# Depthwise-convolution blocks of a Mamba layer: 256-channel halves over four k-tiles, the high and low token parts side by side in one matmul, and the first tap on GpSimd

## The reference

```python
def causal_depthwise_conv(x, w, bias):
    y = lax.conv_general_dilated(x, w[:, None, :], window_strides=(1,),
        padding=[(SSM_CONV - 1, 0)], dimension_numbers=('NWC', 'WIO', 'NWC'),
        feature_group_count=x.shape[-1])
    return y + bias

def mamba2_mixer(proj, conv_w, conv_b, dt_bias, a_log, d_skip, gate_norm):
    z, xbc, dt = jnp.split(proj, [SSM_D_INNER, SSM_D_INNER + SSM_CONV_DIM], axis=-1)
    xbc = jax.nn.silu(causal_depthwise_conv(xbc, conv_w, conv_b))   # 4096 channels, 4 taps
    xs, bm, cm = jnp.split(xbc, [SSM_D_INNER, SSM_D_INNER + SSM_BC], axis=-1)
    dt = jax.nn.softplus(dt + dt_bias)
    ...
```

## Time and profile before

| | |
|---|---|
| median of 3 runs | 1771.86 us (1771.59 to 1771.89) |
| the profiled execution | 1771.1 us, its span 1769.3 us |
| granted TensorE clock | 1.00 over the whole span |
| PE busy | 1763.4 us of the span |
| DVE, ACT, POOL busy | 1162.1, 1004.8, 220.8 us |
| the two convolution stages | 57.8 to 212.4 us (layer 0), 1291.5 to 1446.2 us (layer 3) |

### The profile page before, as it was taken

One profiled execution on the slowest core, in us unless ns is written; L12 is line 12 of the kernel. 1 busy time (PEld: TensorE's weight loads), 2 busy tenths in 40 slices (PEclk: granted clock), 3 DMA queues, 4 the chain that ended last, 5 costly groups with the idle time before them and its releaser, 6 DMA issues.

```text
span 1769.3 us, 25818 instructions
## 1 busy us (share of the span) xinstructions
PE 1763.4 (100%) x9492; PEld 1519.9 (86%) x9492; DVE 1162.1 (66%) x1596; ACT 1004.8 (57%) x1598; POOL 220.8 (12%) x548
## 2 busy tenths in 40 slices
PE   9999999999999999999999999999999999999999
PEld 8998988888888888888888888888899998888887
DVE  5788875655665665666666546666678887556665
ACT  6667775544455675544465545444566777545443
POOL 3412231000012230000012300000131223100000
PEclk9999999999999999999999999999999999999999
DMA  8565543566555443565655445666556554356663
GB/s 285 165 209 183 179 144 124 176 199 191 191 175 176 161 143 119 181 200 190 189 192 196 161 131 174 199 190 193 182 169 205 184 165 156 129 190 191 190 191 131
DMA packets 90041, 314.03 MB, mean 177 GB/s; under 512 B 10176, under 2 KB 11584, under 8 KB 89920
## 3 DMA queue, kind: packets, MB, share of 16 engines
q1 hardware_dynamic: 89328, 311.27, 54.4%
q10 hardware_dynamic: 592, 1.12, 0.2%
HBM read 311.23 MB, written 1.11 MB: 177 GB/s over the span
## 4 chain that ended last, share of the span: by engine, by line
PE 96%; DVE 2%; ACT 1%; issue 0%; DMA 0%; SPq 0%; DVEq 0%; ACTq 0%
PE ps L1229 19%; PE ps L1231 19%; PE ps L1230 19%; PE ps L1251 13%; PE ps L1258 7%; PE ps L1240 3%; PE ps L1241 3%; PE ps L1242 3%; PE ps L1396 2%; PE ps L1376 2%; PE ps L1327 1%; PE ps L1276 1%; PE ps L1286 1%; DVE w_lo_t L1669 1%; DVE xsT L1752 1%; DVE bcT L1752 1%
## 5 line engine op out<-in xcount | busy, mean ns | idle before, releaser
L1669 DVE TENSOR_TENSOR w_lo_t<-raw,w_hi_t 128x1024 fp32r<-128x1024 f32 x569 | 691.9, 1226 | 387.9 <-ACT w_hi_t L1425 387.4
L1425 ACT ACTIVATE w_hi_t<-raw 128x1024 fp32r<-128x1024 f32 x569 | 597.0, 1060 | 394.6 <-PE ps L1231 146.9
L1229 PE MATMUL ps<-w_hi_t,act_hi 128*128 128x512 f32 x832 | 329.2, 396 | 0.0
L1230 PE MATMUL ps<-w_lo_t,act_hi 128*128 128x512 f32 x832 | 324.2, 390 | 0.0
L1231 PE MATMUL ps<-w_hi_t,act_lo 128*128 128x512 f32 x832 | 324.1, 389 | 0.0
L1251 PE MATMUL ps<-hT,w_hi_t 128*128 128x512 f32 x1024 | 256.0, 392 | 0.0
L1251 PEld LDWEIGHTS ps<-hT,w_hi_t 128*128 128x128 f32 x1024 | 185.9, 189 | 34.4
L1231 PEld LDWEIGHTS ps<-w_hi_t,act_lo 128*128 128x128 f32 x832 | 156.2, 188 | 33.1
L1229 PEld LDWEIGHTS ps<-w_hi_t,act_hi 128*128 128x128 f32 x832 | 156.4, 188 | 31.2 <-issue 0.4
L1230 PEld LDWEIGHTS ps<-w_lo_t,act_hi 128*128 128x128 f32 x832 | 156.4, 188 | 30.6
L1229 PE MATMUL ps<-w_hi_t,hT 128*128 128x512 f32 x416 | 165.7, 398 | 0.0
(11 more groups left out here) (219 smaller groups left out, 2220.7 us busy)
## 6 DMA issues: line engine op xcount, KB each, us to landing
raw<-in_wstream SPq DMA_DIRECT2D x569, 512.0 KB, 3.8
gap<-cs_rows SPq DMA_DIRECT2D x32, 256.0 KB, 4.7
mix<-in_mem SPq DMA_DIRECT2D x4, 256.0 KB, 4.9
x<-in_x SPq DMA_DIRECT2D x1, 1024.0 KB, 9.3
raw<-in_wstream SPq DMA_DIRECT2D x2, 256.0 KB, 3.7
wsT<-in_sgu_wT ACTq DMA_DIRECT2D x1, 512.0 KB, 5.4
sgain<-in_sgu_gain ACTq DMA_DIRECT2D x1, 512.0 KB, 6.4
out<-x SPq DMA_DIRECT2D x1, 512.0 KB, 2.8
```

Source lines behind the costliest of these rows:

```text
L1229: pe.matmul(o, ah, wh[:, n], start=first and c == 0, stop=False)
L1230: pe.matmul(o, ah, wl[:, n], start=False, stop=False)
L1425: act.activation(w_hi_t[:, u % RING, :], raw[:, u % RING, :], ACT.Copy).then_inc(w_hi, 1)
L1669: dve.tensor_tensor(w_lo_t[:, u % RING, :], raw[:, u % RING, :], w_hi_t[:, u % RING, :].bitcast(F32), ALU.subtract)\
```

## The change

A block of 512 channels becomes two halves of 256 channels. Each half has two units of four k-tiles (`plan.halves`), form `half`, and takes one of the two pairs of banks; a bank holds one 128-channel tile, high tokens' product in the first 256 columns and low tokens' in the second. A new step `conv_sum` follows each half at once: ACT copies the second halves of the two banks into the new tile `cv`, DVE adds the first halves into `cv` (this frees the banks), and GpSimd multiplies `cv` by the last tap and adds the bias. The step `conv` on DVE then adds the other three taps from `cv` instead of from PSUM, when GpSimd's tap is there. A half unit's weights are loaded by two DMAs of 256 KB with runs of 1 KB instead of one DMA of 512 KB with runs of 4 KB. ACT's two first taps of 256 columns go.

```diff
-            self.block("feat", "hT", w, DIN + ft * P, job, taps)
+            u0 = len(self.units)
+            for half in range(2):
+                job = self.stream_job(True, True)
+                for n in range(2):
+                    u = len(self.units)
+                    self.halves[u] = (u0 + 2 * n, half)
+                    self.unit("half", "hT", (w, 2 * UK * half + UK * n, DIN + ft * P), job, n == 0, n == 1, self.parts["hT"][2 * n + 1], 4 * n,
+                              then=(lambda: half_summed(ft, half, job)) if n else None)
...
+        def half_summed(ft, half, job):
+            if 0 < ft < 16 and half == 0:
+                self.until(lambda: ft // 4 - 1 in xs_act)
+            n = self.count("conv")
+            self.until(lambda: n < 3 or self.n.get("taps", 0) >= n - 2)
+            job.read_act(self)
+            job.read_dve(self)
+            self.step("conv_sum", l=l, ft=ft, half=half, job=job, n=n, xs_free=xs_act[ft // 4 - 1] if 0 < ft < 16 else 0)
+            self.spawn(taps(ft, half, n))
...
+                    for k in range(2):
+                        at = slice(k * UK * 2 * P, (k + 1) * UK * 2 * P)
+                        sp.dma_start(raw[:, u % RING, at].rearrange("p (c f) -> p c f", c=UK),
+                                     A["wstream"][first + k].rearrange("p (c f) -> p c f", c=UK)[:, :, c]).then_inc(raw_in[u % RING], 16)
...
+                elif k == "conv_sum":
+                    h = s["half"]
+                    dst = xsT if s["ft"] < 16 else bcT[:, s["ft"] - 16:s["ft"] - 12, :]
+                    pool.wait_ge(pc_in, 32)
+                    pool.wait_ge(dve_free, s["job"].dve)
+                    if s["xs_free"]:
+                        pool.wait_ge(act_free, s["xs_free"])
+                    for f in range(2):
+                        c = s["l"] * TAPS * 32 + 3 * 32 + s["ft"] + 2 * h + f
+                        ins = pool.tensor_scalar(dst[:, 2 * h + f, :], cv[:, h, f, :], col("conv_w", c), col("conv_b", s["l"] * 32 + s["ft"] + 2 * h + f),
+                                                 ALU.mult, ALU.add)
+                    ins.then_inc(conv_tap, 1)
...
+                    elif s["form"] == "half":
+                        for q in range(4):
+                            for f in range(2):
+                                o, n = ps[:, job.banks[f], :], slice(q * 2 * P + f * P, q * 2 * P + (f + 1) * P)
+                                pe.matmul(o.rearrange("p (a b) -> p a b", a=2), wh[:, n], hT2[:, :, s["at"] + q, :], start=first and q == 0, stop=False,
+                                          skip_group_check=True)
+                        for q in range(4):
+                            for f in range(2):
+                                o, n = ps[:, job.banks[f], :], slice(q * 2 * P + f * P, q * 2 * P + (f + 1) * P)
+                                mm = pe.matmul(o[:, 0:SEQ], wl[:, n], hT2[:, 0, s["at"] + q, :], start=False, stop=last and q == 3,
+                                               skip_group_check=True)
...
-                elif k == "conv":
-                    job, h = s["job"], s["half"]
-                    dst = xsT if s["ft"] < 16 else bcT[:, s["ft"] - 16:s["ft"] - 12, :]
+                elif k == "conv_sum":
+                    job, b = s["job"], s["job"].banks[0]
                     act.wait_ge(job_done, job.done)
...
+                    if s["n"] > 2:
+                        act.wait_ge(conv_done, s["n"] - 2)
+                    act.activation(cv[:, s["half"], :, :], ps[:, b:b + 2, SEQ:2 * SEQ], ACT.Copy).then_inc(act_free, 1)
...
+                elif k == "conv_sum":
+                    job, b, c = s["job"], s["job"].banks[0], cv[:, s["half"], :, :]
+                    dve.wait_ge(act_free, job.act)
+                    dve.tensor_tensor(c, ps[:, b:b + 2, 0:SEQ], c, ALU.add).then_inc(dve_free, 1)
...
+                    dve.wait_ge(conv_tap, s["n"])
                     for d in range(1, TAPS):
```

66 lines of the change are left out of this document (25 added, 41 removed).

## The result

The changed kernel takes **1819.95 us** (median of 4 runs, 1818.5 to 1822.3), the kernel before 1771.82 us on the same chip: a ratio of 1.0274, with a 95% interval of 1.0262 to 1.0287. It is slower, as forecast, but by 48 us where I had forecast 9.5.

What follows compares the result with a forecast made beforehand. PE was taken as the bound, busy 1763.4 of 1769.3 us. A loss of 6.5 us less 1.8 gave +4.7 a layer, +9.5 for two layers on the median of 1771.86: 1781 us, 8-in-10 range 1769 to 1794.

Steps and rivals of the forecast that it cites:

- +6.5 us by unit 33: Layer 0: PE starts unit 33 at about 112.8 us instead of 106.25, as DVE falls behind after waiting for GpSimd.
- -1.8 in the rest of the stage: After unit 33, PE gives back 20 units of 0.09 us, 1.8 us a layer.
- What the change takes from PE: Half units start 2.79 us apart instead of 2.88; 0.09 us a unit over 64 units gives 5.8 us.
- What it adds per half: DVE gains a 0.69 us sum, taps stay 2.60 to 2.68 us, ACT counts 0, POOL's pair takes 1.0 us.
- The new wait: Half 2's tap on POOL stands behind dt_soft, DVE waits for it, and PE waits 4.5 us at unit 25.
- Taps of half 2: On DVE in layer 0, they start once POOL's tap is done, by 81.4 us, and end at 84.05.
- bubbles: DVE's wait for POOL's tap in each half, 1.0 us each, four over halves 3 to 6, 4.0 us.
- my 13.1: Length of dt_soft on POOL: 9.2 us undisturbed, 2.6 from three low parts, 1.3 from taps; ends at 80.3 us.
- the pair of banks: PE needs it for unit 25; half 3's sum on DVE is done at 85.9 us, PE ready at 81.4.
- my 1.3: Half the time of half 1's new two-SBUF-input taps, taken as stretching dt_soft on POOL; range 0 to 2.7 us.
- In the rest of the stage DVE has 16.9 us of idle time: Ten halves' 6.5 us of sums and up to 10 us of bubbles just fit; counted 0, up to 3 us a layer.
- DMA: Half units load as two 256 KB pieces landing in 4.9 us, which fits in some 11 us; counted 0.

Runs made afterwards that it cites:

- e2: Changed kernel with the first tap made by DVE (two tensor_scalar) and nothing of the convolution on GpSimd: 1822.1 us.
- e9: Changed kernel with a third bank pair for blocks 16 and 8, keys' turns on banks 4 and 5, SSD groups 4 to 7 at old units, single load: 1795.3 us.
- e11: e9 with the first tap made by DVE instead of GpSimd: 1795.2 us.
- e13: e11 with the silu of a bc block 1 unit earlier and an SSD group's squares 1 unit later in ACT's list: 1779.0 us.
- e5: Changed kernel with the last of DVE's three taps left out, so the output is not the reference's: 1802.8 us.
- e6: Kernel before the change with only its SSD steps moved to the changed kernel's units: 1787.8 us.
- e7: Changed kernel with its SSD steps put back at the units they had before the change: 1814.5 us.
- e3: Changed kernel with a half unit's weights laid out as one 4 KB run a partition and loaded by one 512 KB transfer: 1815.0 us.

## Why the prediction was right in sign and wrong in size

The forecast was +6.5 us by unit 33 and -1.8 in the rest of the stage, 4.7 a layer. Measured in layer 0: +5.3 by unit 33, +13.1 from there to the end of the stage at unit 65, and +6.6 behind the stage, for which the sum had no term. That the kernel is slower came out as forecast, but in the main not by the forecast mechanism: GpSimd's tap accounts for at most 2.7 of the 5.3 us at unit 33 (e2), and without it the kernel is no faster. In this the right sign was luck.

1. **What the change takes from PE: right.** A half unit's matmuls take 2.79 us, and in every stretch without a wait the delay falls by 0.08 to 0.09 us a unit (from 3.94 us at unit 20 to 3.27 at unit 28).
2. **What it adds per half: right but for one term.** The sum has a mean of 684 ns, POOL's pair is 1.10 us. The taps, which I took as unchanged, are 2.70 us where GpSimd is idle. Where GpSimd's SSD products run beside them they are longer, and GpSimd's own pair is longer beside DVE's work (changed kernel, POOL and DVE):

```profile
124.70 3.13 POOL L1175 TENSOR_SCALAR xsT<-cv,percol_sb 128x256 f32<-128x256 f32 x2 [7.71 <-issue]
```

```profile
127.87 3.99 DVE L1788 SCALAR_TENSOR_TENSOR xsT<-cv,percol_sb,xsT 128x255 f32<-128x255 f32 x6 [0.46 <-POOL xsT L1175]
```

3. **The new wait: right in its mechanism, and hidden.** Taps of half 2 at 81.39 us (forecast 81.4), bubbles of 1.00 us (forecast 1.0), delay at unit 33 of 5.3 us (forecast 6.5). Both close figures are partly luck. In the first two errors cancel: `dt_soft` began at 67.87 us, 0.7 later than forecast, and took 12.4 us for my 13.1. In the last, 4.4 us came from another stop, at unit 19. e9 shows the forecast one, a wait of 3.6 us for 4.5 with 1.5 us of slower matmuls behind it, which the sum did not have; e11 shows that GpSimd was its cause. By the Trainium skill, page "SBUF — State Buffer", section "Who interferes with whom", the new taps should have stretched `dt_soft`. They did, but little: of the six instructions beside them five took 0.36 to 0.51 us, the like ones later 0.32 to 0.37, some 0.4 us in all against my 1.3.
4. **The first step that failed: "The new wait", where "the pair of banks" is asked for at unit 25 alone.** I followed the pair of the halves' own sums. I did not ask who had filled a pair before and who empties it. A block of four units leaves the reader of the other pair four units; a half leaves it two. The reader of a normed block is squares, a chain of some 5 us on GpSimd and a product on DVE. That is 4.4 us at unit 19, 6.3 at unit 55.
5. **The second: "In the rest of the stage DVE has 16.9 us of idle time ... This just fits ... I count 0, with up to 3 us".** The idle time was there, and DVE's sum of work did fit: e11 has more of it and is level with the kernel before at unit 49. But an in-order list doesn't let idle time be used where it isn't. DVE late at `cbm` holds ACT, ACT holds the casts. This is 5.7 us by unit 54 (e13 leaves 0.8 of it, e5 0.7).
6. **The third: I read the plan for the first stretch only.** The change moves the SSD steps of groups 4 to 7 by up to 4 units later and some of groups 1 to 3 by up to 2 earlier. e6 measures the new places alone: 16 us on the kernel before. I had this in the order of the two kernels and did not price it. In the changed kernel the share of it that can be told apart is the 6.0 us a layer behind unit 65; taking all of it back there (e7) gives only 5.5 us in both layers.
7. **DMA: counted at 0, measured at 5 us** (e3). The median landing is short, 3.5 us a piece, yet ACT's casts wait 13.8 us for weights, against 1.4 with one transfer. That this happens where DVE frees a slot late is my reading, not shown. Whether it is the second issue or the shorter runs was not isolated; e3 changes both.
8. **The clock: not counted.** PE's pace after a stop is the lower one for the 16 matmuls that follow (2.97 and 1.82 us for 2.00 and 1.11). Of 2.8 us of stop it makes 4.4 us of delay. It is part of the losses above, and I could not take it apart from them but for unit 19 (1.6 us) and e9's unit 25 (1.5 us).

The sum in layer 0 by unit 91: 5.3 until unit 33, 0.6 to 49, 5.7 to 54, 6.3 at 55, 1.3 to 60, 0.8 given back to 65, 6.0 to 91: 24.4 us. It is 25.0 by the end of the layer, and with 24.1 in layer 3 the growth of the profiled span, 49.7 us, is accounted for but for 0.6. What stays open: whether a plan exists that hides both what e13 loses behind unit 54 and the GpSimd chain at unit 66. It was not tried. Open is also how the 1.3 us behind unit 55 and the 0.6 between 33 and 49 come about.

## What to carry to other kernels

When a buffer is handed on twice as often, list for each use who filled it last and how long its *slowest* reader takes; the average reader hides it. Idle time of an engine with an in-order list is no reserve for work added elsewhere in the list: look at what stands behind each instruction that waits for this engine, above all the casts or loads that feed the bottleneck. A cost in a planner is part of the change: run the old kernel with the new order, and the new kernel with the old one, before anything else is blamed.
